# A fused two-block kernel on one core: four units projected ahead of the root, taps of two halves in turn, parts made straight from the sum

## What is computed, cut to what matters

```python
u = rms_norm(h, norm1_g[l])            # h * rsqrt(mean(h*h) + eps) * gain
h = h + mixer_layer(u, w_in[l], ...)
v = rms_norm(h, norm2_g[l])
h = h + hier_moe(v, ...)
...
p = u @ w_in                           # in the mixer
a, bv, bg, q, k, v, fg, gates = jnp.split(p, ...)
glu = bv * jax.nn.sigmoid(bg)          # 256 channels
y = lax.conv_general_dilated(glu, conv_w...)   # causal, 31 taps, each channel by itself
y = layer_norm(y + conv_b, ln_g, ln_b)
```

## Time and profile before

| | |
|---|---|
| median of 3 runs (lowest, highest) | 2081.35 us (2080.3, 2086.7) |
| the profiled execution: its time, its span | 2079.4 us, 2077.6 us |
| PE busy | 1985.2 us, 96% |
| DVE busy | 1427.2 us, 69% |
| ACT busy | 964.7 us, 46% |
| mean granted TensorE clock | 0.985 |
| PE in the 40 slices of the page | 5 in the first, 7 in the 18th, 9 or 8 in nearly all others |

### The profile page before, as it was taken

The page is one execution under the profiler, slowest core; times in us unless marked ns, Lnnn a source line. Parts: engine busy times, 40 slices in busy tenths (PEclk is TensorE's granted clock), DMA queues, the critical chain, the costliest instruction groups (busy, mean ns, idle before and its releaser), DMA issues.

```text
span 2077.6 us, 26689 instructions
## 1 busy us (share of the span) xinstructions
PE 1985.2 (96%) x8972; PEld 1567.6 (75%) x8972; DVE 1427.2 (69%) x2200; ACT 964.7 (46%) x1402; POOL 26.2 (1%) x46
## 2 busy tenths in 40 slices
PE   5999999989999999999999999999998999999997
PEld 5987888877776777766667788888875678888885
DVE  5995534566999874857756888874387578888533
ACT  4566433446777424456664433333255453333321
POOL 0000000001000000000000000000011000000000
PEclk9999999999999999989999999999999999999998
DMA  4220233225999235400002232333331033232332
GB/s 159 83 71 11 92 91 100 92 92 210 355 353 340 99 92 160 125 1 1 1 1 78 86 100 91 92 100 102 110 112 47 1 109 94 91 99 93 101 101 81
DMA packets 65272, 219.05 MB, mean 105 GB/s; under 512 B 9440, under 2 KB 10624, under 8 KB 65056
## 3 DMA queue, kind: packets, MB, share of 16 engines
q1 hardware_dynamic: 59856, 210.77, 30.8%
q10 hardware_dynamic: 5328, 7.15, 1.3%
HBM read 209.04 MB, written 2.10 MB: 102 GB/s over the span
## 4 chain that ended last, share of the span: by engine, by line
PE 76%; DVE 15%; ACT 4%; issue 3%; DMA 1%; ACTq 1%; DVEq 0%; SPq 0%
PE psum L934 52%; PE psum L1334 5%; PE psum L1505 3%; DVE w_lo L2586 2%; DVE sig L2809 2%; PE psum L1260 2%; PE psum L1307 1%; PE psum L1641 1%; PE psum L1488 1%; PE psum L1486 1%; PE psum L1317 1%; PE psum L1096 1%; PE psum L1441 1%; PE psum L1502 1%; PE psum L1388 1%
## 5 line engine op out<-in xcount | busy, mean ns | idle before, releaser
L934 PE MATMUL psum<-x_hi,w_hi 128*128 128x512 f32 (+1 forms) x1408 | 513.1, 378 | 15.7 <-DVE x_lo L2620 6.6
L934 PE MATMUL psum<-x_lo,w_hi 128*128 128x512 f32 (+1 forms) x1408 | 512.1, 378 | 0.0
L934 PE MATMUL psum<-x_hi,w_lo 128*128 128x512 f32 (+1 forms) x1408 | 509.4, 376 | 0.0
L2586 DVE TENSOR_TENSOR w_lo<-raw,w_hi 128x1024 fp32r<-128x1024 f32 x243 | 296.5, 1222 | 194.7 <-ACT w_hi L1740 193.8
L1740 ACT ACTIVATE w_hi<-raw 128x1024 fp32r<-128x1024 f32 x243 | 255.7, 1054 | 193.2 <-DMA raw<-stream 192.6
L934 PEld LDWEIGHTS psum<-x_hi,w_hi 128*128 128x128 f32 x1408 | 258.1, 189 | 72.9 <-issue 9.1
L934 PEld LDWEIGHTS psum<-x_lo,w_hi 128*128 128x128 f32 x1408 | 257.5, 189 | 51.8 <-issue 1.4
L934 PEld LDWEIGHTS psum<-x_hi,w_lo 128*128 128x128 f32 x1408 | 257.9, 189 | 49.9
L934 PE MATMUL psum<-hid_hi,w_hi 128*128 128x512 f32 x624 | 244.8, 392 | 2.2 <-DVE w_lo L2586 1.4
L934 PE MATMUL psum<-hid_lo,w_hi 128*128 128x512 f32 x624 | 244.5, 392 | 0.0
L934 PE MATMUL psum<-hid_hi,w_lo 128*128 128x512 f32 x624 | 243.9, 391 | 0.0
(11 more groups left out here) (608 smaller groups left out, 3015.9 us busy)
## 6 DMA issues: line engine op xcount, KB each, us to landing
raw<-stream SPq DMA_DIRECT2D x251, 512.0 KB, 3.5
raw<-experts SPq DMA_DIRECT2D x70, 512.0 KB, 5.3
raw_more<-experts SPq DMA_DIRECT2D x68, 512.0 KB, 5.3
staged<-staged ACTq DMA_DIRECT2D x84, 64.0 KB, 3.0
resid<-x_fm SPq DMA_DIRECT2D x4, 528.0 KB, 6.9
out_fm<-resid SPq DMA_DIRECT2D x4, 512.0 KB, 2.9
consts<-consts_in SPq DMA_DIRECT2D x1, 1373.0 KB, 14.1
kv_pairs<-kv_even_odd ACTq DMA_DIRECT2D x4, 256.0 KB, 4.1
```

The source lines that it names most:

```text
L934: last = pe.matmul(o, wt[:, slot, k * P:(k + 1) * P], m[part], start=start and p == 0, stop=stop and p == 2, skip_group_check=True)
L2586: dve.tensor_tensor(w_lo[:, slot, :], raw[:, slot, :], w_hi[:, slot, :].bitcast(F32), ALU.subtract)\
```

## The change

It has three parts.

1. **The opening.** SP's order becomes: norm1's gain alone (the first 8 columns of vecs), x's first two chunks, units 0 and 1, the rest of x, the ones matrix, the rest of vecs, units 2 and 3. ACT makes high parts of x times gain, without the root, into `o_hi`; DVE makes the low parts in one instruction (x times gain minus the high part) into `o_lo`. bv's and bg's four units run on these. The sum of squares stands on PE in front of the last two chunks of bv. DVE multiplies the root into the four results as it reads them from PSUM (`rooted`); ACT's sigmoid becomes an instruction of its own, on SBUF. `normed` still makes the rooted parts in XH/XL, for pool and later units, now behind bv. The adding of squares goes into two sums.
2. **The convolution.** Tap k of the first 128 channels, then tap k of the second 128, and so on. Before each tap DVE waits for the tap before of the same channels, which stands two instructions back. `amid` keeps its indices, counted over the 62 taps in the new order.
3. **Residual seams.** ACT makes the high part from the residual sum itself, with the gain as its scale, ahead of the square; DVE makes the low part in one instruction from the sum, the gain and the high part. The multiplication into scratch is gone.

```diff
@@ SP
-            sp.dma_start(vecs[:, :], vecs_in).then_inc(vecs_loaded, 16)
+            sp.dma_start(vecs[:, 0:C], vecs_in[:, 0:C]).then_inc(x_loaded[0], 16)
+            sp.dma_start(H[:, 0:2, :], x_in[:, 0:2, :]).then_inc(x_loaded[0], 16)
+            for s in range(2):
+                sp.dma_start(raw[:, s, :], stream[s, :, :]).then_inc(raw_loaded[s], 16)
+            for i in range(1, 4):
+                sp.dma_start(H[:, 2 * i:2 * i + 2, :], x_in[:, 2 * i:2 * i + 2, :]).then_inc(x_loaded[i], 16)
             sp.dma_start(consts[:, 0:2 * P], consts_in[:, 0:2 * P]).then_inc(ones_loaded, 16)
-            for i in range(4):
...
+            sp.dma_start(vecs[:, C:], vecs_in[:, C:]).then_inc(vecs_loaded, 16)
+            for s in range(2, SLOTS):
@@ PE
                 for k in range(KC):
+                    if late_sum and k == KC - 2:
+                        late_sum()
...
-            gathered_sum("n1", T1)
+            def early_x(k):
+                return o_hi(k, T1), o_lo(k, T1)
...
-            two_units(U["bv"], r, T1, x_of(T1), (x_ready, X0["n1"]))
+            two_units(U["bv"], r, T1, early_x, (x_ready, X0["early"]), first_sum)
             for n in range(U["bg"], U["v1"]):
-                unit(n, n % SLOTS, r + n - U["bv"], (r + n - U["bv"]) % PAIRS, T1, x_of(T1))
+                early = n < U["bg"] + 2
+                unit(n, n % SLOTS, r + n - U["bv"], (r + n - U["bv"]) % PAIRS, T1, early_x if early else x_of(T1),
+                     (x_ready, X0["n1"]) if n == U["bg"] + 2 else None)
@@ ACT, residual
                     act.wait_ge(ev_used, E0[name] + c + 1)
+                    if gain:
+                        act.activation(XH[:, c, T1 - t:T1], H[:, c, T1 - t:T1], ACT.Copy, scale=vec(gain, c)).then_inc(hi_ready, 1)
                     if c >= 2:
...
-                    if scaled:
-
-                        act.wait_ge(y_ready, X0[norm] + c + 1)
-                        act.activation(XH[:, c, T1 - t:T1], TS[:, c % 2, 0:t], ACT.Copy).then_inc(hi_ready, 1)
@@ ACT, opening
+            act.wait_ge(x_loaded[0], 32)
             for c in range(C):
...
+                act.activation(o_hi(c, T1), H[:, c, :], ACT.Copy, scale=vec("norm1", c)).then_inc(hi_ready, 1)
+                if c == 0:
+                    high_weights(0)
+                    high_weights(1)
...
                 act.activation(first_squares(c), H[:, c, :], ACT.Square).then_inc(sq_ready, 1)
...
+            root_table()
+            high_weights(2)
+            high_weights(3)
             root("n1", R["n1"], T1, D)
...
+            def gate_values(c):
+
+                act.wait_ge(lin_free, r + 2 + c + 1)
+                act.activation(sig[:, c, :], sig[:, c, :], ACT.Sigmoid).then_inc(act_done, 1)
+
+            high_parts(X0["n1"], T1, x_hi(T1), {0: lambda: high_weights(4)})
+            high_weights(5)
+            for c in range(2):
+                gate_values(c)
+            high_weights(6)
@@ DVE, residual
                         dve.wait_ge(ev_used, E0[name] + c + 1)
-                        dve.wait_ge(x_ready, x - 1)
-                        dve.tensor_scalar(TS[:, c % 2, 0:t], h, vec(gain, c), None, ALU.mult).then_inc(y_ready, 1)
-
-                        dve.wait_ge(hi_ready, x + 1)
-                        dve.tensor_tensor(XL[:, c, T1 - t:T1], TS[:, c % 2, 0:t], XH[:, c, T1 - t:T1].bitcast(F32),
-                                          ALU.subtract).then_inc(x_ready, 1)
+                        dve.wait_ge(hi_ready, X0[norm] + c + 1)
+                        dve.scalar_tensor_tensor(out=XL[:, c, T1 - t:T1], in0=h, scalar=vec(gain, c), in1=XH[:, c, T1 - t:T1].bitcast(F32),
+                                                 op0=ALU.mult, op1=ALU.subtract).then_inc(x_ready, 1)
@@ DVE, opening
+            def first_sum(c):
...
+                dve.tensor_tensor(SQ[:, c % 2, :], SQ[:, c % 2, :], first_squares(c), ALU.add).then_inc(sq_added, 1)
+
+            for c in range(C):
+
+                dve.wait_ge(x_loaded[c // 2], 32 if c < 2 else 16)
+                dve.wait_ge(hi_ready, X0["early"] + c + 1)
+                dve.scalar_tensor_tensor(out=o_lo(c, T1), in0=H[:, c, :], scalar=vec("norm1", c), in1=o_hi(c, T1).bitcast(F32),
+                                         op0=ALU.mult, op1=ALU.subtract).then_inc(x_ready, 1)
+                if c == 0:
+                    for n in range(2):
+                        low_weights(n)
+                if c > 2:
+                    first_sum(c - 1)
+            first_sum(C - 1)
+            low_weights(2)
+            low_weights(3)
+            reciprocal_root(R["n1"], T1)
+
+            def rooted(c, out_):
+
+                dve.wait_ge(unit_used, U["bv"] + c + 1)
+                dve.tensor_tensor(halves(out_), pair(R["in1"] + c)[:, :, 0:HALF], halves(TS[:, 2, :]), ALU.mult).then_inc(lin_free, 1)
+
+            dve.wait_ge(pads_zeroed, 7)
+            for c in range(2):
+                rooted(c, glu[:, c, KS - 1:KS - 1 + T1])
+            normed("norm1", X0["n1"], T1, x_hi(T1), x_lo(T1), 0, {1: lambda: rooted(2, sig[:, 0, :]), 2: lambda: low_weights(4)})
+            rooted(3, sig[:, 1, :])
@@ DVE, convolution
-            for n in range(SLOTS, SLOTS + 3):
+            for n in range(SLOTS + 1, SLOTS + 3):
                 low_weights(n)
-            dve.wait_ge(lin_free, R["in1"] + 4)
+            dve.wait_ge(act_done, DONE0["bg"] + 2)
...
-                for k in range(1, KS):
-                    ins = dve.scalar_tensor_tensor(out=y, in0=glu[:, c, k + META:k + T1], scalar=vec("conv_w", c * KS + k), in1=y,
-                                                   op0=ALU.mult, op1=ALU.add)
+            tap_done = [0, 0]
+            for k in range(KS):
+                for c in range(2):
...
+                        dve.wait_ge(dve_step, tap_done[c])
+                        ins = dve.scalar_tensor_tensor(out=y, in0=glu[:, c, k + META:k + T1], scalar=vec("conv_w", c * KS + k), in1=y,
+                                                       op0=ALU.mult, op1=ALU.add)
...
-                        then(ins)
+                        steps[0] = steps[0] + 1
+                        tap_done[c] = steps[0]
+                        ins.then_inc(dve_step, 1)
...
-                    if c * KS + k in amid:
-                        amid[c * KS + k]()
+                    if 2 * k + c in amid:
+                        amid[2 * k + c]()
```

More of the change, by code:

```diff
@@ L191 @@
     N_ALONE += _count
-X0 = {"n1": 0, "n2": C, "na0": 2 * C, "nf0": 3 * C, "na1": 4 * C, "nf_1": 5 * C}
+X0 = {_name: _i * C for _i, _name in enumerate(("early", "n1", "n2", "na0", "nf0", "na1", "nf_1"))}
+Y0 = {"n1": 0, "na0": C}
 HID0 = {"pool": 0, "conv": 2, "merge": 4, "ffn0": 12, "ffn1": 12 + FC}
@@ L1814, in h_of, with residual @@
                 return lambda c: H[:, c, T1 - t:T1]
-            def residual(name, t, norm, units=1, scaled=False, early=0):
+            def residual(name, t, norm, gain=None, units=1, early=0):
                 root_table()
@@ L1881, in _ @@
                 act.activation(first_squares(c), H[:, c, :], ACT.Square).then_inc(sq_ready, 1)
-            for n in range(2):
-                high_weights(n)
+            act.wait_ge(vecs_loaded, 16)
+            root_table()
+            high_weights(2)
+            high_weights(3)
             root("n1", R["n1"], T1, D)
-            high_parts(X0["n1"], T1, x_hi(T1))
-            for n in range(2, SLOTS):
-                high_weights(n)
             r, n = R["in1"], U["bv"]
-            for c in range(6):
-                by_unit(n + c)
-                if c < 2:
-                    evacuate((r + c) % PAIRS, glu[:, c, KS - 1:KS - 1 + T1], T1)
-                elif c < 4:
-                    evacuate((r + c) % PAIRS, sig[:, c - 2, :], T1, ACT.Sigmoid)
-                else:
-                    evacuate((r + c) % PAIRS, apad[:, c - 4, 16:16 + T1], T1)
-                if c:
-                    high_weights(n + c + AHEAD)
+            def gate_values(c):
[6 more added lines that the diff above has]
+            high_weights(6)
+            for c in range(4, 6):
+                by_unit(n + c)
+                evacuate((r + c) % PAIRS, apad[:, c - 4, 16:16 + T1], T1)
+                high_weights(n + c + AHEAD)
             by_unit(U["fg"])
@@ L2402, in _ @@
             output_parts(PAIRS2 - 1)
-            residual("wo2", T2, "nf0", scaled=True, early=1)
+            residual("wo2", T2, "nf0", "ffn0", early=1)
             root("nf0", R["nf0"], T2, D)
@@ L2555, in _ @@
                 window_output_high(p)
-            residual("wo3", T2, "nf_1", scaled=True, early=1)
+            residual("wo3", T2, "nf_1", "ffn1", early=1)
             root("nf_1", R["nf_1"], T2, D)
@@ L2603, in reciprocal_root, with normed @@
                 then(dve.reciprocal(TS[:, 2, 0:t], TS[:, 2, 0:t]))
-            def normed(gain, count0, t, hi, lo, used):
+            def normed(gain, count0, t, hi, lo, used, after={}):
                 if used:
@@ L2730, in _ @@
```

(35 more changed lines are left out.)

39 lines of the change are left out of this document (20 added, 19 removed).

## The result

The changed kernel takes 2058.97 us (median of 4 runs, 2057.86 to 2062.81), the kernel before 2081.73 us: a ratio of 0.989, 95% interval 0.9876 to 0.9904, 22.8 us less. I had forecast 2062.6 us, 18.7 us less, and a range of 2059.5 to 2069.5. The profiled execution took 2057.86 us, with a span of 2056.1 us.

What follows compares the result with a forecast made beforehand. PE was taken to bound the kernel (76% of the span); 14.9 us from opening and convolution plus 3.8 from seams took 2079.4 to 2060.7, and 1.95 to the median gave 2062.6 us. Range 2060 to 2066, with two rivals 2059.5 to 2069.5.

Steps and rivals of the forecast that it cites:

- PE's start: Opening: PE starts units at 11.2 us after unit 1 lands at 8.8; bg ends at 37.9, 14.2 us earlier.
- DVE to the first tap: Opening: DVE's work after the reciprocal puts the convolution's first tap at 47.6 us, where it was 56.2.
- Taps: Convolution: waiting two back cuts the pitch from 0.785 to 0.67 us, saving 6.6 us; it ends at 116.4 us.
- Merge units: After the convolution: opening and taps together make the sum over the channels end 14.9 us earlier, at 117.9 us.
- Seams: Residual seams: PE's low-part waits go, 3.0 us, plus 0.4 each at wo2 and wo3: 3.8 us.
- The sum: Whole kernel: 14.9 us from opening and convolution plus 3.8 us from the seams, 18.7 us less.
- All rivals: Two-back waits save nothing, 2068.9 us, chance 0.12; late start, 2066.6, 0.15; gain lost later, 2077.6, 0.04; low clock, 2090.2, 0.03.
- From there every engine goes on in its old order, DVE 15 us earlier too, so I let it stand: After the convolution's channel sum: the 14.9 us lead was taken to stand unchanged through the rest of the kernel.
- the step from a difference of two spans to a median: Whole kernel: 18.7 us off the profiled 2079.4 gives 2060.7; adding 1.95 us for the median gives 2062.6 us.

Runs made afterwards that it cites:

- the seams alone: The kernel before with only the low and high parts at the residual seams made straight from the sum, opening and taps as before: 2075.74 us.
- fillers in both: Throwaway matmuls in PE's idle places, and PE's wait before wo2 and wo3 moved ahead, added to changed kernel and kernel before: 2056.34 and 2075.74 us.
- the high part of unit 6 first: The changed kernel with ACT making the high part of unit 6's weights before the two sigmoids: 2058.03 us.
- three filled places: The changed kernel with unit 6's high part before the sigmoids, PE's wo2/wo3 waits moved ahead, throwaway matmuls at 85, 434 and 740 us: 2051.88 us.

## Why the prediction was right, and where it failed

**PE's start.** Forecast 11.2 us, measured 9.94. Unit 1 had landed at 2.1 + 5.4 = 7.5 us, not 8.8. The slow matmuls at the start lasted until 15.4 us, 5.4 us and not about 3. The two errors cancel, which is luck: the sum of squares started at 21.35 us (21.2) without a wait, and bg ended at 37.8 (37.9).

**DVE to the first tap.** Reciprocal 24.06 us (23.7), wait for w_hi of unit 6 1.54 (1.4), first tap 47.99 (47.6). Right. The multiplication out of PSUM is 1.32 us for two, 0.66 each (0.70).

**Taps.** Pitch 0.66 us (0.67), last tap at 116.01 (116.4), unit 11 at 87.72 (87.8). The number is right; its cause is split, 5.5 us by the distance and 2.0 by where the wait stands. What the Trainium skill ("VectorE: DVE Perf Modes", "The DRAIN you can't avoid") measured on copies, that a semaphore after each costs nothing, does not carry over to a chain in which each instruction waits: seven taps take 5.47 us with the wait one back and 4.72 with it two back.

**Merge units.** Forecast 14.9 us ahead, measured 14.04. Unit 15 ended 0.3 us later than forecast. The other 0.6 us: I let only the second half's sum over the channels stand behind unit 15 and the last tap. Before, the first half's sum ran while PE waited for that tap; with alternating halves both sums, 0.86 us each, follow unit 15.

**Seams.** Forecast 3.8 us (1.0 at each of three and 0.4 at wo2 and wo3), measured 4.1 in the trace of the whole change, 4.35 in that of the seams alone, 3.6 at equal clock. The split was off: 1.27 us at each of the three, 0.3 at wo3's gap and 0.14 at wo2's.

**The sum.** 18.7 us were forecast; 18.1 show in the trace at the edited places, 19.4 with fillers in both, 20.0 at equal clock. All rivals have fallen: the pitch is 0.66 us, PE started early and not late, PE's clock rose at 15.4 us, and the lead of 14 us stands until 740 us.

**What failed** is the step "From there every engine goes on in its old order, DVE 15 us earlier too, so I let it stand", and with it the step from a difference of two spans to a median. That put what the clock does at the unedited places at nothing. The order is the old one, but PE arrives at its idle places at another moment, and how long the granted clock stays low behind them differs from execution to execution and from kernel to kernel. In the profiled pair the edited places gave 18.2 us, these places 2.7 and the wait near 1100 us 0.6, so the spans differ by 21.5 and not by 18.7. Then I added 1.95 us to come from the profiled execution to the median; for the changed kernel that distance was 1.1 us. The two together, 2.8 and 0.8 us, are the distance between 2062.6 and 2058.97. Neither the sum nor the range had a term for this; the lower bound should have been some 3 us lower.

Over all executions the mean clock was 0.984 before (44) and 0.987 after (8), 0.0034 apart: 3.2 us by the slope. About half of it has a plain place. Before, PE stood idle from 20.5 to 27.1 us, and the granted clock was 0.50 behind it; the changed kernel has no such place:

```profile
25.00:30.00 5.00, 2.91 (x13) 2.94 (x14) 4.86 (x8) 2.57 (x4) 0.00 (x0) 0.50 0.00 0
```

That half was in the forecast, which took PE's start from there; only the rest was not. Why the other places fall differently is open. The fillers at the gather and at 740 us show that PE's idleness in front of a place matters, not what sets the moment.

## What to carry to other kernels

Before pricing an edit, list the places where PE stands idle, edited or not, with the granted clock behind each; here the ones that cost were idle for 2 to 4.3 us. They belong in the range of the forecast. In this kernel three of them, filled with 11 throwaway matmuls, gave 6 us together with a move that alone had given nothing that could be told. When two halves of a computation are independent, alternate them so that each wait is for the instruction two back, and put the wait at the consumer. A part that saves time on one engine is worth only what the other engine can follow; run the parts alone and together to see it.

## What the runs showed of the hardware

- The first pairs of matmuls, from 9.94 to 15.4 us, take 0.64 us with overlap, and 0.41 from 15.73 us on. The windows of the profile read 1.00 all the while, but the trace has no entry of the granted clock before 15.6 us, and a stretch without an entry reads as full. With the seams alone the first entry stands at 31.7 us, and the pairs take 0.64 us from 27.6 until then. So the column says nothing of the time before its first entry; the length of the matmuls does.
- Behind a gap of 2.6 us at 85 us the clock fell in the other profiled execution of the changed kernel, which lost 1.2 us there, and with the high part of unit 6 first; it stayed up in the first profile of the changed kernel: the same code, either way.
- Not every fall follows idleness. Near 466 us (three filled places) PE is busy with 32 matmuls of 36 columns, and the pairs behind them are slow (1.05 us, later 0.62). The same fall stands behind the same instructions in the profile before (at 484 us), in the changed kernel's (at 470 us) and in all the others:

```profile
462.39 3.67 PE L1312 MATMUL psum<-comb_parts,slot_of_token 128*128 128x36 f32 x32
466.13 1.19 PE L1361 MATMUL psum<-w_hi,x_cell_even 128*128 128x512 f32 x2
```

- A wait one instruction back costs DVE 0.12 us an instruction (0.785 against 0.66 us); an instruction whose wait is already met starts 0.07 to 0.09 us before its forerunner ends.
